# The first modulation group laid out by output columns in four parts, and three units begun chunk by chunk while it loads

## The chip, the cores and the metric

The kernel runs on one core of a Trainium2 chip. The metric is the device time of one execution in microseconds (us). Three runs of the kernel before gave 2286.52, 2291.09 and 2291.59 us, median 2291.09 us. The execution that the profiler recorded took 2286.39 us, of which 2284.6 us are the span of its instructions.

## The reference, cut to what matters

The reference is two stacks of transformer layers on 256 tokens of width 1024: two layers of a first kind, then two of a second. The change touches the beginning of the first layer alone:

```
c_act = silu(c)                                     # one vector of 1024
mod   = c_act @ w_mod[l] + b_mod[l]                 # [1024] @ [1024, 6144]
sh1, sc1, g1, sh2, sc2, g2 = split(mod, 6)
h = rms(x, ln1[l]) * (1 + sc1) + sh1                # x is [256, 1024]
p = h @ w_in[l]                                     # then heads, attention, output projection
```

So nothing of `h` can be had before `sh1` and `sc1` (the first 2048 columns of `mod`, 8 MB of float32 weights), and nothing of `p` before `h`. Each element of `h` in chunk k (128 of the 1024 features) needs only the 128 columns of `sh1` and the 128 columns of `sc1` that belong to chunk k, but over all 1024 rows of `w_mod`.

## The kernel before, in words

Activations lie transposed: features on the 128 partitions, in KC = 8 chunks, and the T = 256 tokens along the free axis. Weights come as **units**, 128 output columns by all 1024 rows (512 KB). A unit is loaded in two halves (the two queue entries of `unit(v)`, L1699) into RAW, which holds two units; ScalarE makes its high part WH, half by half (`split_high`, L2178); VectorE makes the low part WL of the first half (`split_low`, L2436) and GpSimd that of the second (`low`, L1778). A unit's product is then 24 matmuls: WH by the high and the low part of `h`, and WL by the high part. The ring of WH and WL holds four units. The loads are all issued by SyncE (SP) in one written order, and each load waits there until what lies in its place has been used: unit v waits until units up to v-2 have both low parts (`lo_done` at least v-1, half by half), from unit 2 on; nothing behind it in the list is issued before.

**The modulation.** Its weights are read in steps of 128 rows by 2048 columns, each in two halves of 512 KB. One group is 8 steps: 2048 output columns. In `modulate` (L1849) a half gives two matmuls of 512 columns, each with the 32-wide stationary operand `c_act` of its chunk repeated, so that the four matmuls of a step write four strips of 32 partitions of PSUM bank 7. `extract` (L2507) turns the bank with one transpose, adds the bias (L2516) and makes the gains A1 (L2526). The halves 0 to 15, the leading group, have places of their own in SBUF and need not wait. Halves 16 and 17 stand on SP's list behind unit 5, and TensorE uses them (`modulate` of step 8) behind unit 3.

**The beginning of the first layer, before.** SP issues: the vectors c, halves 0 to 3, common constants, x, parameters P1, halves 4 to 11, units 0 and 1, halves 12 to 15, then units 2 and 3, the large constants (1088 KB) and unit 4 and so on. TensorE: the modulation of halves 0 to 3, the sum of squares (`norm_sums`, L1950, 8 matmuls in float32), halves 4 to 15, then `units_begun` for units 0 and 1 (L1882, L1883, and L1888 with the low part of `h`), unit 2, the first rotation (L2004), unit 3, step 8 of the modulation, and the pair of units 4 and 5. ScalarE: squares of x (L2233), the root (L2227, L2229), the high parts of units 0 and 1, the eight chunks of the high part of `h` (H1, L2247), then the high parts of units 2 and 3. VectorE: the refinement of the root (L2463 to L2467), the low parts of units 0 and 1, `extract(0)`, the eight scaled chunks (L2497), and the eight low chunks of `h` (L2493), with the low part of unit 2 behind chunk 3 and that of unit 3 behind chunk 7.

A float32 matmul is shown as two records of two passes each; the matmuls of the units are one pass and one record.

Of the kernel before, what the change touches and what calls it, by code (L numbers as in the profile page):

```python
# [57 lines left out]
BEGINNING = (2, 3)  # L58
# [85 lines left out]
def build(nc, stream, mods, consts, consts2, par1, par2, lam, ccols, xT, ctxT, outT):  # L144
# [147 lines left out]
    late_full = lead_full[4:]  # L292
    mod_used, group_read, mods_ready = (sem(n) for n in ("mod_used", "group_read", "mods_ready"))
# [1373 lines left out]
    def _(sp):  # L1667
        def modulation(s):

            for half in range(2):  # L1670
                modulation_half(2 * s + half)

# [51 lines left out]
        for s in range(2):  # L1724
            modulation(s)
        sp.dma_start(C[:, 0:COMMON_W], consts[:, 0:COMMON_W]).then_inc(common_in, 16)
        sp.dma_start(X, xT).then_inc(x_in, 16)
        sp.dma_start(P1[:, :, :], par1).then_inc(common_in, 16)
        for s in range(2, LEAD - 2):
            modulation(s)  # L1730
        for v in range(2):
            unit(v)
        for s in range(LEAD - 2, LEAD):
            modulation(s)
        for l in range(DEPTH):
            for v in range(PER):
                if l or v >= 4:
                    unit(l * PER + v)
                for h in halves_behind(l, v):
                    modulation_half(h)  # L1740
                if l == 0 and v == 1:
                    for x in (2, 3):
                        unit(x)
                    sp.dma_start(C[:, COMMON_W:COMMON_W + FIRST_W], consts[:, COMMON_W:]).then_inc(consts_in, 16)
                if l == 0 and v == IN_UNITS + WO_UNITS + 1:
                    sp.dma_start(P2[:, :, :], par2).then_inc(later_in, 16)
                if l == DEPTH - 1 and v == IN_UNITS + WO_UNITS + 24:
# [73 lines left out]
    def _(pe):  # L1821
        def modulate(s):
# [6 lines left out]
            for half in range(2):  # L1829
# [21 lines left out]
                last.then_inc(mod_used, 1)  # L1851
        def unit_wait(base, i, j):
# [85 lines left out]
        def first_layer(l):  # L1938
# [3 lines left out]
            def norm_sums(half):  # L1942
                index = 2 * l + half
                pe.wait_ge(common_in, 32)
                if index:
                    pe.wait_ge(sq_added, index)
                    pe.matmul(PS[:, 6, 0:T], ones, SQ[:, 0, :], start=True, stop=False)
                for k in range(KC - 1 if index else 0, KC):
                    pe.wait_ge(sq_done, index * KC + k + 1)
                    last = pe.matmul(PS[:, 6, 0:T], ones, SQ[:, k, :], start=(k == 0), stop=(k == KC - 1))  # L1950
                last.then_inc(sum_done, 1)

            if l == 0:
                for s in range(2):
                    modulate(s)
            norm_sums(0)
            for s in range(NORM_STEPS):
                if l:
                    modulate(at + s)
            if l == 0:  # L1960
                for s in range(2, LEAD):
                    modulate(s)
# [56 lines left out]
            for x in range(IN_UNITS):  # L2019
                if x in (VALUES, VALUES + 2):  # L2020
                    token_pair(base, 0, x, H1, 0, 2)
                elif x == 0:
                    units_begun([(base + y, H1, T) for y in range(BEGINNING[l])], 2 * l)
                elif x >= BEGINNING[l] and not VALUES < x < VALUES + 4:
                    unit(x)
                if x == 2:
                    if l == 0:
                        pe.wait_ge(consts_in, 16)
                    rotate(0)
# [140 lines left out]
    def _(act):  # L2170
# [64 lines left out]
        def norm(l, half):  # L2235
# [5 lines left out]
            if half == 0 and l == 0:  # L2241
                for u in range(2):
                    split_high(u, 0, 1)
# [185 lines left out]
    def _(dve):  # L2429
# [51 lines left out]
        def norm(l, half):  # L2481
            dve.wait_ge(rstd_done, 2 * l + half + 1)
            refined(RS[:, 1, :], RS[:, 0, :], PS[:, 6, 0:T], 1.0 / D)
            if l == 0 and half == 0:
                for u in range(2):
                    split_low(u, 0, 1)
                dve.wait_ge(common_in, 32)
                extract(0)

# [6 lines left out]
            for k in range(KC):  # L2496
                dve.scalar_tensor_tensor(NX[:, k, :], X[:, k, :], A1[:, l, half, k:k + 1], RS[:, 1, :],  # L2497
                                         ALU.mult, ALU.mult).then_inc(nx_done, 1)
            for k in range(KC):
                low(k)  # L2500
                if l == 0 and half == 0 and k % 4 == 3:
                    split_low(2 + k // 4, 0, 1)
# [80 lines left out]
        def first_layer(l):  # L2583
# [76 lines left out]
            for x in range(IN_UNITS):  # L2660
                next_low(base, 0, x)
                if x == 2:
# [301 lines left out]
def _modulations(a):  # L2964
# [3 lines left out]
    steps = strips.transpose(2, 0, 1, 4, 3, 5).reshape(STEPS, P, 4, 4 * P)  # L2968
    rows = np.ascontiguousarray(a["w_mod"][1].T).reshape(BESIDE * KC, 2, P, D).transpose(0, 2, 1, 3)
# [61 lines left out]
```

## Time and profile before

| | us |
|---|---|
| three runs | 2286.52, 2291.09, 2291.59 |
| profiled execution, its own time | 2286.39 |
| its span | 2284.6 |
| TensorE busy | 2208.7 (97%) |
| VectorE / ScalarE / GpSimd busy | 1258.5 / 1109.8 / 726.9 |

The page gives each engine's busy time over the span, the busy share in 40 slices, the queues, and the chain of work that ended last. The first slice of TensorE is the only one under 80% (7 tenths). The change lies within the first 60 us, so the rows below come mostly from there: the timeline (start, duration, engine, line, operation, what was written and read, count, and in brackets the idle time before it and what released it), and the table of windows.

### The profile page before, as it was taken

Reading aid. Unit: us, or ns where it says so; the run is one execution under the profiler, and the core shown is the slowest. Engines: PE = TensorE matmul, PEld = TensorE weight load, DVE = VectorE, ACT = ScalarE, POOL = GpSimd, SP = SyncE. Lnnn points to the kernel's source line nnn. Section 1 sums busy time; section 2 is a strip of 40 time slices with the busy share of each in tenths; the row PEclk is TensorE's granted clock in tenths of the full one; section 3 lists DMA queues with packets and bytes.
Section 4 is the critical chain, followed back from the end, with each engine's and each line's share of the span. In section 5 each row is a group of like instructions: output and inputs, shape, how many; then the busy total and the mean of one; then the engine's idle time right before and its main releaser. Section 6 shows DMA issues by size and latency. Waiting matters only on the chain.

```text
span 2284.6 us, 41129 instructions
## 1 busy us (share of the span) xinstructions
PE 2208.7 (97%) x14780; PEld 1931.1 (85%) x14780; DVE 1258.5 (55%) x2278; ACT 1109.8 (49%) x2323; POOL 726.9 (32%) x563
## 2 busy tenths in 40 slices
PE   7999999999999999999999999999989999999999
PEld 4869998869998888878887688888879889787999
DVE  3767668776446645531344764363465664437564
ACT  3465554565455444532355653232343665647553
POOL 2404554414664221122221012222223235221443
PEclk9999999999999999999999999999999999999999
DMA  8766997675775322123222113223223335222554
GB/s 304 233 236 216 321 333 295 207 258 172 243 241 175 93 83 65 56 87 93 79 74 70 33 47 101 92 65 101 92 74 116 101 114 168 83 84 65 168 162 148
DMA packets 159893, 328.47 MB, mean 144 GB/s; under 512 B 17808, under 2 KB 21136, under 8 KB 159632
## 3 DMA queue, kind: packets, MB, share of 16 engines
q1 hardware_dynamic: 159616, 325.80, 43.6%
q8 instruction: 89, 1.46, 0.3%
q0 software_dynamic: 144, 0.85, 0.1%
q14 instruction: 44, 0.36, 0.1%
HBM read 325.53 MB, written 1.05 MB: 143 GB/s over the span
## 4 chain that ended last, share of the span: by engine, by line
PE 78%; issue 8%; DVE 5%; POOL 4%; ACT 2%; DMA 1%; SPq 1%; POOLq 0%; DVEq 0%; ACTq 0%
PE PS L1868 16%; PE PS L1869 15%; PE PS L1870 15%; PE PS L1913 4%; PE PS L1915 4%; PE PS L1914 4%; POOL WL L1778 3%; PE PS L737 2%; PE PS L717 2%; PE PS L1849 1%; POOL AR L1798 1%; PE PS L1932 1%; PE PS L1931 1%; PE PS L1930 1%; PE PS L751 1%
## 5 line engine op out<-in xcount | busy, mean ns | idle before, releaser
L1778 POOL TENSOR_TENSOR WL<-RAW,WH 128x512 fp32r<-128x512 f32 x434 | 598.2, 1379 | 1453.6 <-ACT WH L2178 1301.3
L1868 PE MATMUL PS<-AR,WH 128*128 128x256 f32 (+1 forms) x2632 | 857.4, 326 | 4.0 <-DVE AR L1626 1.9
L1869 PE MATMUL PS<-AR,WH 128*128 128x256 f32 (+1 forms) x2632 | 844.5, 321 | 0.0
L1870 PE MATMUL PS<-AR,WL 128*128 128x256 f32 (+1 forms) x2632 | 843.8, 321 | 0.0
L2178 ACT ACTIVATE WH<-RAW 128x512 fp32r<-128x512 f32 x840 | 492.0, 626 | 326.2 <-PE PS L1870 172.3
L2436 DVE TENSOR_TENSOR WL<-RAW,WH 128x512 fp32r<-128x512 f32 x434 | 357.2, 823 | 454.2 <-ACT WH L2178 452.2
L1868 PEld LDWEIGHTS PS<-AR,WH 128*128 128x128 f32 x2632 | 496.5, 189 | 54.6 <-issue 8.1
L1869 PEld LDWEIGHTS PS<-AR,WH 128*128 128x128 f32 x2632 | 496.8, 189 | 41.3 <-issue 2.4
L1870 PEld LDWEIGHTS PS<-AR,WL 128*128 128x128 f32 x2632 | 496.7, 189 | 40.0
L1913 PE MATMUL PS<-WH,AR 128*128 128x256 f32 x768 | 219.3, 286 | 0.0
L1915 PE MATMUL PS<-WH,AR 128*128 128x256 f32 x768 | 216.2, 282 | 0.0
L1914 PE MATMUL PS<-WL,AR 128*128 128x256 f32 x768 | 216.1, 281 | 0.0
L1913 PEld LDWEIGHTS PS<-WH,AR 128*128 128x128 f32 x768 | 144.6, 188 | 3.6 <-issue 3.0
L1914 PEld LDWEIGHTS PS<-WL,AR 128*128 128x128 f32 x768 | 144.7, 188 | 0.7 <-issue 0.5
L1915 PEld LDWEIGHTS PS<-WH,AR 128*128 128x128 f32 x768 | 144.5, 188 | 0.0
L1931 PE MATMUL PS<-AR,WH 128*128 128x256 f32 x352 | 99.1, 281 | 0.0
L1930 PE MATMUL PS<-AR,WH 128*128 128x256 f32 x352 | 99.1, 281 | 0.0
L1932 PE MATMUL PS<-AR,WL 128*128 128x256 f32 x352 | 99.0, 281 | 0.0
L1038 ACT ACTIVATE WORK<-PS 128x512 f32<-128x512 f32 (+1 forms) x48 | 23.5, 490 | 129.8 <-PE PS L1870 129.6
L1100 ACT ACTIVATE WORK<-PS,BC,QN 128x512 f32<-128x512 f32 (+1 forms) x96 | 66.9, 705 | 8.8 <-DVE BC L1502 8.8
L1500 DVE TENSOR_REDUCE BC<-PS 128x2 f32<-128x1024 f32 (+1 forms) x48 | 50.1, 1044 | 36.0 <-PE PS L717 36.0
L1932 PEld LDWEIGHTS PS<-AR,WL 128*128 128x128 f32 x352 | 66.3, 188 | 0.0
(309 smaller groups left out, 3060.9 us busy)
## 6 DMA issues: line engine op xcount, KB each, us to landing
RAW<-stream SPq DMA_DIRECT2D x868, 256.0 KB, 3.0
WORK<-mods SPq DMA_DIRECT2D x144, 512.0 KB, 5.9
WORK<-stream SPq DMA_DIRECT2D x68, 256.0 KB, 5.1
C<-consts SPq DMA_DIRECT2D x1, 1088.0 KB, 7.4
XX<-xT SPq DMA_DIRECT2D x1, 1024.0 KB, 10.2
XX<-ctxT SPq DMA_DIRECT2D x1, 1024.0 KB, 7.3
outT<-XX SPq DMA_DIRECT2D x8, 128.0 KB, 1.9
C<-consts POOLq DMA_DIRECT2D x1, 832.0 KB, 7.0
```

Source lines behind the costliest of these rows:

```text
L1778: pool.tensor_tensor(WL[:, u % 4, cut, :], raw(u, 1), WH[:, u % 4, cut, :].bitcast(f32), ALU.subtract).then_inc(lo_done[1], 1)
L1868: pe.matmul(out, WH[:, u % 4, k, :], moving[:, 0, k, :], start=(k == 0), stop=False)
L1869: pe.matmul(out, WH[:, u % 4, k, :], moving[:, 1, k, :], start=False, stop=False)
L1870: last = pe.matmul(out, WL[:, u % 4, k, :], moving[:, 0, k, :], start=False, stop=(k == KC - 1))
L1913: pe.matmul(out, still[:, 0, k, cut], WH[:, both, k, :], start=(k == 0), stop=False)
L1914: pe.matmul(out, still[:, 0, k, cut], WL[:, both, k, :], start=False, stop=False)
L1915: last = pe.matmul(out, still[:, 1, k, cut], WH[:, both, k, :], start=False, stop=(k == KC - 1))
L1930: pe.matmul(PS[:, b, 0:T], WH[:, u % 4, k, :], HID[:, 0, kk, :], start=(kk == 0), stop=False)
L1931: pe.matmul(PS[:, b, 0:T], WH[:, u % 4, k, :], HID[:, 1, kk, :], start=False, stop=False)
L1932: last = pe.matmul(PS[:, b, 0:T], WL[:, u % 4, k, :], HID[:, 0, kk, :], start=False, stop=(kk == FC - 1))
L2178: act.activation(WH[:, u % 4, cut, :], raw(u, half), ACT.Copy).then_inc(hi_done, 1)
L2436: dve.tensor_tensor(WL[:, u % 4, cut, :], raw(u, 0), WH[:, u % 4, cut, :].bitcast(f32), ALU.subtract).then_inc(lo_done[0], 1)
```

## The change

The weights of the leading group are laid out anew in memory: in four parts of four halves, where part p holds the columns of chunks 2p and 2p+1 of `sh1` and `sc1` (512 columns) over all 1024 rows. So each half holds two row chunks of 512 columns, and each gives eight matmuls of 128 columns, four per row chunk, in place of two of 512. Each part has a PSUM bank (7, 4, 5, 7), a transpose of 128 by 128, and its own small additions.

```
-BEGINNING = (2, 3)
+BEGINNING = (3, 3)
+PAIRS = KC // 2
+PAIR_BANK = (7, 4, 5, 7)
+BEHIND_CHUNK = {1: (0, 1), 3: (2,), 7: (3,)}
...
 SP:
-        for s in range(2):
-            modulation(s)
+        sp.dma_start(X, xT).then_inc(x_in, 16)
         sp.dma_start(C[:, 0:COMMON_W], consts[:, 0:COMMON_W]).then_inc(common_in, 16)
-        sp.dma_start(X, xT).then_inc(x_in, 16)
         sp.dma_start(P1[:, :, :], par1).then_inc(common_in, 16)
-        for s in range(2, LEAD - 2):
-            modulation(s)
-        for v in range(2):
-            unit(v)
-        for s in range(LEAD - 2, LEAD):
-            modulation(s)
+        for p, behind in enumerate(((0, 1), (2,), (), (3,))):
+            for h in range(4 * p, 4 * p + 4):
+                modulation_half(h)
+            for v in behind:
+                unit(v)
...
                 if l == 0 and v == 1:
-                    for x in (2, 3):
-                        unit(x)
...
 TensorE:
+        def pair(p):
+            if p == PAIRS - 1:
+                pe.wait_ge(pair_read, 1)
+            for h in range(4 * p, 4 * p + 4):
+                if h < 4:
+                    pe.wait_ge(mod_full[h], 16)
+                else:
+                    pe.wait_ge(lead_full[h - 4], 16)
+                for x in range(2):
+                    k = 2 * (h % 4) + x
+                    still = CA[:, 0, k:k + 1].broadcast_to([P, STRIP])
+                    for a in range(4):
+                        last = pe.matmul(PS[a * STRIP:(a + 1) * STRIP, PAIR_BANK[p], 0:P], still,
+                                         LEADING[h][:, x, a * P:(a + 1) * P], start=(k == 0), stop=(k == KC - 1))
+                last.then_inc(mod_used, 1)
+
+        def start_chunk(u, k):
+            if k == 0:
+                unit_wait(u, 0, 0)
+            pe.wait_ge(nhi_done, k + 1)
+            out = PS[:, u, 0:T]
+            pe.matmul(out, WH[:, u, k, :], H1[:, 0, k, :], start=(k == 0), stop=False)
+            pe.matmul(out, WL[:, u, k, :], H1[:, 0, k, :], start=False, stop=False)
+            pe.wait_ge(norm_done, k + 1)
+            return pe.matmul(out, WH[:, u, k, :], H1[:, 1, k, :], start=False, stop=(k == KC - 1))
+
+        def start():
+            norm_sums_first()
+            pair(0)
+            pair(1)
+            for k in (0, 1):
+                for u in (0, 1):
+                    start_chunk(u, k)
+            pair(2)
+            for k in (0, 1):
+                start_chunk(2, k)
+            for k in (2, 3, 4, 5):
+                for u in range(3):
+                    start_chunk(u, k)
+            pair(3)
+            for u in range(3):
+                for k in (6, 7):
+                    last = start_chunk(u, k)
+                last.then_inc(unit_done, 1)
...
+                elif x == 0 and l == 0:
+                    start()
...
-                if x == 2:
+                if x == (2 if l else 3):
                     if l == 0:
                         pe.wait_ge(consts_in, 16)
                     rotate(0)
...
 ScalarE, norm(0, 0):
-            if half == 0 and l == 0:
-                for u in range(2):
-                    split_high(u, 0, 1)
             for k in range(KC):
                 ... (the high part of chunk k)
-            if half == 0 and l == 0:
-                for u in range(2, 4):
-                    split_high(u, 0, 1)
+                if half == 0 and l == 0:
+                    for u in BEHIND_CHUNK.get(k, ()):
+                        split_high(u, 0, 1)
...
 VectorE, norm(0, 0), behind the refinement of the root:
+            if l == 0 and half == 0:
+                dve.wait_ge(common_in, 32)
+                for p in range(PAIRS):
+                    pair_columns(p)
+                    for k in (2 * p, 2 * p + 1):
+                        scaled(k)
+                    for k in (2 * p, 2 * p + 1):
+                        low(k)
+                        for u in BEHIND_CHUNK.get(k, ()):
+                            split_low(u, 0, 1)
+                return
...
+        def pair_columns(p):
+            dve.wait_ge(mod_used, 4 * (p + 1))
+            ... (transpose of 128x128 out of PAIR_BANK[p], the bias added to 2x2 columns, 2 columns of A1)
```

`norm_sums_first` is the sum of squares as before. GpSimd's list is unchanged. VectorE's first `rope(0)` moves behind the low part of one more unit, as the rotation does on TensorE; in the second layer (l = 1) nothing changes.

## Rows read from the trace of the kernel before

**Rows 1.** The page: span, TensorE's busy time, and the ending chain by engine.

```profile
span 2284.6 us, 41129 instructions
...
PE 2208.7 (97%) x14780; PEld 1931.1 (85%) x14780; DVE 1258.5 (55%) x2278; ACT 1109.8 (49%) x2323; POOL 726.9 (32%) x563
...
PE 78%; issue 8%; DVE 5%; POOL 4%; ACT 2%; DMA 1%; SPq 1%; POOLq 0%; DVEq 0%; ACTq 0%
```

**Rows 2.** Timeline of the first 35 us, all engines.

```profile
13.91 2.56 ACT L2233 ACTIVATE WORK<-XX 128x256 f32<-128x256 f32 x8 [11.30 <-DMA XX<-xT]
...
14.47 5.38 PE L1950 MATMUL PS<-WORK,C 128*128 128x256 f32 x16 [3.08 <-ACT WORK L2233]
...
19.78 3.05 PE L1849 MATMUL PS<-WORK,CA 128*32 128x512 f32 x24
...
21.76 0.43 DVE L2467 SCALAR_TENSOR_TENSOR WORK<-WORK 128x256 f32<-128x256 f32 x1
...
26.25 2.94 POOL L1778 TENSOR_TENSOR WL<-RAW,WH 128x512 fp32r<-128x512 f32 x2 [25.80 <-ACT WH L2178]
...
28.11 4.88 PE L1849 MATMUL PS<-WORK,CA 128*32 128x512 f32 x16 [2.73 <-DMA WORK<-mods]
...
31.93 0.14 PEld L1849 LDWEIGHTS PS<-WORK,CA 128*32 128x32 f32 x4 [1.08 <-DMA WORK<-mods]
33.11 0.72 DVE L2507 STREAM_TRANSPOSE WORK<-PS 128x512 f32<-128x512 f32 x1 [5.04 <-PE PS L1849]
...
34.28 3.25 DVE L2497 SCALAR_TENSOR_TENSOR WORK<-XX,A,WORK 128x256 f32<-128x256 f32 x8
34.80 3.30 ACT L2247 ACTIVATE AR<-WORK,M 128x256 fp32r<-128x256 f32 x8 [7.37 <-DVE WORK L2497]
```

**Rows 3.** Timeline from 35 to 47 us, all engines.

```profile
35.45 0.55 PE L1882 MATMUL PS<-AR,WH 128*128 128x256 f32 x1 [2.46 <-ACT AR L2247]
...
38.57 0.37 PE L1882 MATMUL PS<-AR,WH 128*128 128x256 f32 x1
...
39.21 3.06 POOL L1778 TENSOR_TENSOR WL<-RAW,WH 128x512 fp32r<-128x512 f32 x2 [10.02 <-ACT WH L2178]
...
39.64 3.71 DVE L2493 SCALAR_TENSOR_TENSOR AR<-WORK,M,AR 128x256 fp32r<-128x256 f32 x4
...
43.28 0.68 DVE L2436 TENSOR_TENSOR WL<-RAW,WH 128x512 fp32r<-128x512 f32 x1
...
44.11 1.14 ACT L2178 ACTIVATE WH<-RAW 128x512 fp32r<-128x512 f32 x2
```

**Rows 4.** SP's queue in the timeline: issues of loads.

```profile
39.75 0.33 SPq L1699 DMA_DIRECT2D RAW<-stream  x1
...
43.98 0.80 SPq L1699 DMA_DIRECT2D RAW<-stream  x2
...
45.30 0.43 SPq L1689 DMA_DIRECT2D WORK<-mods  x1
```

**Rows 5.** Timeline of TensorE around step 8 of the modulation.

```profile
50.94 0.28 PE L1869 MATMUL PS<-AR,WH 128*128 128x256 f32 x1
51.05 0.28 PE L1870 MATMUL PS<-AR,WL 128*128 128x256 f32 x1
51.26 1.05 PE L1849 MATMUL PS<-WORK,CA 128*32 128x512 f32 x4
52.50 1.05 PE L1849 MATMUL PS<-WORK,CA 128*32 128x512 f32 x4 [0.18 <-DMA WORK<-mods]
53.48 0.39 PE L1913 MATMUL PS<-WH,AR 128*128 128x256 f32 x1
```

**Rows 6.** Windows of TensorE alone: us, busy (records), granted clock, DMA share, GB/s.

```profile
29.30:31.90 2.60, 2.60 (x10) 0.50 1.02 403
...
37.00:38.50 1.50, 1.50 (x9) 0.50 0.00 0
```

**Rows 7.** Timeline of TensorE: a burst of very small matmuls in a later layer.

```profile
797.75 1.15 PE L551 MATMUL PS<-C,WORK 4*128 4x4 f32 x16
```

More of the change, by code:

```diff
@@ L292, in build @@
     late_full = lead_full[4:]
+    pair_read = sem("pair_read")
     mod_used, group_read, mods_ready = (sem(n) for n in ("mod_used", "group_read", "mods_ready"))
@@ L1667, in _ @@
     def _(sp):
-        def modulation(s):
-            for half in range(2):
-                modulation_half(2 * s + half)
         def modulation_half(h):
@@ L1851, in modulate, with norm_sums_first @@
                 last.then_inc(mod_used, 1)
+        def pair(p):
[40 more added lines that the diff above has]
+                last.then_inc(unit_done, 1)
+        def norm_sums_first():
+            pe.wait_ge(common_in, 32)
+            for k in range(KC):
+                pe.wait_ge(sq_done, k + 1)
+                last = pe.matmul(PS[:, 6, 0:T], ones, SQ[:, k, :], start=(k == 0), stop=(k == KC - 1))
+            last.then_inc(sum_done, 1)
         def unit_wait(base, i, j):
@@ L1943, in norm_sums @@
                 index = 2 * l + half
[L1944 to L1958, printed above, removed]
+                pe.wait_ge(sq_added, index)
+                pe.matmul(PS[:, 6, 0:T], ones, SQ[:, 0, :], start=True, stop=False)
+                pe.wait_ge(sq_done, index * KC + KC)
+                pe.matmul(PS[:, 6, 0:T], ones, SQ[:, KC - 1, :], start=False, stop=True).then_inc(sum_done, 1)
+            if l:
+                norm_sums(0)
+                for s in range(NORM_STEPS):
                     modulate(at + s)
-            if l == 0:
-                for s in range(2, LEAD):
-                    modulate(s)
             def unit(x):
@@ L2483, in norm @@
             refined(RS[:, 1, :], RS[:, 0, :], PS[:, 6, 0:T], 1.0 / D)
[L2484 to L2488, printed above, removed]
             def low(k):
@@ L2494, in low, with scaled @@
                                          H1[:, 0, k, :].bitcast(f32), ALU.add, ALU.subtract).then_inc(norm_done, 1)
-            for k in range(KC):
+            def scaled(k):
                 dve.scalar_tensor_tensor(NX[:, k, :], X[:, k, :], A1[:, l, half, k:k + 1], RS[:, 1, :],
                                          ALU.mult, ALU.mult).then_inc(nx_done, 1)
+            if l == 0 and half == 0:
[9 more added lines that the diff above has]
+                return
+            for k in range(KC):
+                scaled(k)
             for k in range(KC):
                 low(k)
-                if l == 0 and half == 0 and k % 4 == 3:
-                    split_low(2 + k // 4, 0, 1)
+        def pair_columns(p):
+            dve.wait_ge(mod_used, 4 * (p + 1))
+            columns, bank = slice(4 * p, 4 * p + 4), PAIR_BANK[p]
+            turned = dve.transpose(MT[:, columns, :].rearrange("p m r -> p (m r)"), PS[:, bank, 0:P])
+            if p < PAIRS - 1:
+                turned.then_inc(pair_read, 1)
+                dve.wait_ge(pair_read, p + 1)
+            else:
+                turned.then_inc(group_read, 1)
+                dve.wait_ge(group_read, 1)
+            cut, bias, gain = slice(2 * p, 2 * p + 2), PAR1["bmod"], PAR1["ln1"] + 2 * p
+            halves = lambda x: x.rearrange("p (h k) -> p h k", h=2)
+            chain(dve.tensor_tensor(halves(M1[:, 0, 0:16])[:, :, cut], halves(MT[:, columns, 0]),
+                                    halves(P1[:, 0, bias:bias + 16])[:, :, cut], ALU.add))
+            chain.wait()
+            chain(dve.scalar_tensor_tensor(A1[:, 0, 0, cut], M1[:, 0, KC + 2 * p:KC + 2 * p + 2], 1.0,
+                                           P1[:, 0, gain:gain + 2], ALU.add, ALU.mult))
+            chain.wait()
         def extract(g):
@@ L2661, in first_layer @@
                 next_low(base, 0, x)
-                if x == 2:
+                if x == (2 if l else 3):
                     rope(0)
@@ L2968, in _modulations @@
     steps = strips.transpose(2, 0, 1, 4, 3, 5).reshape(STEPS, P, 4, 4 * P)
+    pairs = wide[:, 0:2 * D].reshape(PAIRS, 2, P, 2, PAIRS, 2, 4, STRIP).transpose(4, 0, 2, 1, 6, 3, 5, 7)
+    steps[0:KC] = pairs.reshape(2 * KC, P, 2, 4 * P).reshape(KC, 2, P, 2, 4 * P).transpose(
+        0, 2, 1, 3, 4).reshape(KC, P, 4, 4 * P)
     rows = np.ascontiguousarray(a["w_mod"][1].T).reshape(BESIDE * KC, 2, P, D).transpose(0, 2, 1, 3)
```

## The prediction

> **What bounds the kernel now.** The page comes first: 97% of the span TensorE is busy and 78% of the ending chain is its own work [rows 1], so a change must take time out of TensorE's list or let it start earlier. Then the timeline of the first 60 us. TensorE does no matmul of a unit before 35.45 us [rows 3]. Until 33.0 it waits for the leading modulation group: halves 12 to 15 arrive 1.27 us apart (28.11 to 31.93, three steps), and the windows show 403 GB/s at a DMA share of 1.02 [rows 2, 6]. That stretch is bound by the transfers. From 33.11 the chain is serial: one transpose and two small operations until 34.28, eight scaled chunks, and from 35.45 the matmuls of units 0 and 1, at the half rate of TensorE's clock (granted 0.50) [rows 2, 3, 6]. Then the low chunks: four of them take 3.71 us, 0.93 each, beside GpSimd's low parts of units 2 and 3 [rows 3]. The last wait that decides in this beginning is further on: half 17, issued at 45.30 behind unit 5, is used at 52.50 with 0.18 us of idle time before it, and the pair of units 4 and 5 starts at 53.48 behind it [rows 4, 5]. Unit 5 in turn was held on SP until VectorE had made the low part of unit 3 (43.28 to 43.96) [rows 3, 4]. So two things must come earlier: TensorE's units, and the low part of unit 3 with the loads behind it.
>
> **The loads.** The same bytes move, in another order. In front of half 15 stands one unit more (unit 2, 512 KB, as much as a half): 31.93 + 1.27 = 33.2 us. Counting back at 1.27: half 11 at 28.1, unit 2 at 23.0, half 7 at 21.8, half 3 at 14.2; x, now first, by about 6 and the parameters by 8 instead of 14.4 (bounds 6 and 10; the sums move with them, but half 3 does not). SP now stands at unit 2 until the low part of unit 0 is made, with halves 8 to 15 behind it. That part: sums of squares 8.0 + 5.4 = 13.4; the refined root 2.3 later, as now (19.85 to 22.2), 15.7; first part's columns 0.7 (below), two scaled chunks and their high parts, 17.7; the high part of unit 0, 0.57 a half, 18.8; GpSimd's low part 1.5, 20.4 [rows 2, 3]. What has been issued by then keeps the queues busy until 23.0, so I take this wait at nothing, with 2 us of cover. If the cover is gone, every us of delay moves halves 8 to 15, and all behind them, by one.
>
> **TensorE's modulation.** Before, a step of four matmuls on four strips takes 3.05/3 = 1.02 us [rows 2]; the strips run side by side. After, a row chunk is the same four strips with 128 columns, a quarter: 0.26 us, 2.0 us a part, 8.2 in all, as before, but in 128 matmuls instead of 32. Below the arrival rate (0.5 us a half against 1.27). The other end: the burst of small matmuls has 16 records in 1.15 us, 0.07 each [rows 7]; a row chunk has 8 records, 0.57 us, 4.6 a part, still below 1.27 a half, but 2.6 us later where a part's data lie waiting. I take 0.26, the nearer row: the same operation with the same operands. The Trainium skill has a rule for each end (TensorE: Matmul & The Clock Gate, "Wait — 56ns, not 53.3ns?"): a start-to-start floor of about 25 ns, and about 62 ns a matmul where the sequencer decodes in software. By the first the part would take an estimated 1.7 us, by the second 4.0. No row shows 128 columns on four strips, so the trace decides nothing between them yet.
>
> **TensorE between parts 2 and 3.** Part 2 is done at 28.1 + 0.6 = 28.7, at the half rate 29.0. Then 6 matmuls of unit 2 and 36 of chunks 2 to 5. At the half rate a matmul takes (38.57 - 35.45)/14 = 0.22 us, at the full one 0.12 (50.94 to 51.05) [rows 3, 5]. Before, the clock stood at 0.50 in this same place (29.3 to 31.9) and rose after some 3 us of work, in both places where it was low [rows 6, 3]. So 14 matmuls at 0.22 and 28 at 0.12: 6.4 us, until 35.3 (all at full rate: 33.7; all low: 38.2). Chunks 4 and 5 are ready at 31.5 and wait for nobody. Part 3 lies ready since 33.2: 2.0 us. **End of part 3, E = 37.3** (35.6 to 40.2; with the 0.57 of above 39.9).
>
> **Behind E.** The transpose of 128 by 128 is between nothing and the 0.72 of 128 by 512; I take 0.3. With the two small operations (34.28 - 33.11 - 0.72 = 0.45) the columns cost 0.75. Two scaled chunks at 0.41 and the high part of chunk 7 end at E + 2.1, its low part at E + 2.6 [rows 2]. The matmuls behind it (12 of units 1 and 2, at 0.12 to 0.22) end at E + 4.2 to 5.3. Unit 3: high parts E + 2.1 to 3.2, GpSimd's low part, 1.3 to 1.5 us, at E + 4.7 [rows 3]. So unit 3 runs from about E + 4.9 = 42.2 to 45.1, and the rotation until 45.6. Before, unit 3 ended at 51.2 [rows 5]. So far 6 us would be won.
>
> **What is late next.** Behind unit 3 comes step 8 of the modulation, with halves 16 and 17. SP issues them behind unit 5, whose second half waits for GpSimd's low part of unit 3, E + 4.7. So half 17 goes out at E + 5.7 = 43.0, against 45.30: 2.3 us earlier, not 6. It took 7.2 us from there to its use [rows 4, 5], and the loads around it (unit 5, unit 6 and half 16) are the same at about the same distances, so I leave it at 7.2: 50.2, against 52.50. TensorE stands idle from 45.6 until half 16 comes, about 49, and again a little before half 17. Idle stretches of 2.5 us and more stand before both low stretches of the clock here (12.0 to 14.4 and 33.0 to 35.4 [rows 2, 3]), so I expect the matmuls behind to start at the half rate: between 0 and 14 matmuls of the pair at 0.22 instead of 0.12 and up to 0.9 us in half 17's own matmuls; 0.8 taken. Gain at the start of the pair: 2.3 - 0.8 = **1.5 us**.
>
> **What remains.** From there on every wait is relative to TensorE (evictions, low parts, the issues behind them), and I find no load that is due at a fixed time; the gain stays as it is. The first rotation moved costs nothing: it stood on TensorE's path before (0.43 us, between units 2 and 3), now it lies in the wait for half 16. On VectorE the rope behind it is one low part later, with more than 4 us until it is needed by the key scores. The low chunks 6 and 7 no longer run beside GpSimd: 0.41 instead of 0.93, inside the sum. Sum against the profiled execution: 2286.4 - 1.5 = 2284.9. The median of the runs shown lies 4.7 us above that execution, so 2291.1 - 1.5 = **2289.6 us**. About 0.2% (4.6 us) is what a measurement of this kernel can tell from no change.
>
> **Rivals.**
>
> A. *The gain comes through.* Clock at full rate behind part 2 (E = 35.6), and half 17 lands after 5 us instead of 7.2. For it: the queues lie idle for some us before (0 to 2 loads outstanding), so little stands in front. Against it: 7.2 us was measured with an idle queue before it too (windows after 37.0 show 0 GB/s [rows 6]). Gain 2.3 + 1.7 + 2.2 = 6.2 without cooling, 5 to 6 us: 2285.5.
>
> B. *Slower: SP stuck at unit 2.* One mechanism: the low part of unit 0 comes later than about 21 us, the queues run dry, and halves 8 to 15 are late. For it: the chain to it is long (x, sums at the half rate, root, a part's columns, ScalarE's halves), each term from a row in another setting; if the matmuls of part 0 go at 0.57 a chunk it comes 2 us later by itself, and part 3 takes 2.6 more. Against it: 2 us of cover. Price: E later by the delay beyond the cover; the gain of 1.5 is gone from 1.5 us of delay on. With 2 us of delay and 2.6 in part 3: 3.1 us slower, 2294.2. The pace of 62 ns in the skill's page, above, would lead here.
>
> C. *Nothing.* The half-rate clock lasts longer than 14 matmuls behind part 2 and again behind the idle time (E = 38.5, 1.5 us of cooling): 2291.0.
>
> D. *It does not do what it says*: the units are begun early, but part 3 stands behind the 42 matmuls in TensorE's order, and with all of them at the low rate E is 40.2, no earlier than the units' end is now: 0.6 us lost at half 17 and 0.8 by the clock, 1.4 us slower, 2292.5.
>
> **From this the numbers.** Forecast (gain 0.5 to 3.5) 0.45; A 0.2; B 0.17; C 0.1; D 0.08. Faster by over 0.2%: nearly all of A and a little of the forecast where the gain reaches its end, 0.22. Slower by over 0.2%: B where its delays add up, and the tail of D, 0.14. Within: 0.64. Range: from A's 2285.5 to B's 2294.2, drawn in by half a us above for the tails left out: 2285.0 to 2293.8.
>
> **What would show it.** Right: half 15 used near 33.2 with no hole in the DMA share between 20 and 33; matmuls of units 0 and 1 from about 22; a row chunk of the modulation at 0.26; part 3 behind 42 unit matmuls, E near 37; TensorE idle for 3 us before step 8 with the wait on the mods; half 17 issued near 43. Wrong: a DMA share well under 1 around 23 us (B); no idle time before step 8 (A, then the gain is 5 us or more); a clock at 1.00 throughout 28 to 36; or a pair of units 4 and 5 that starts before 49 us.

## The result, and the profile after

The kernel after takes 2294.39 us (median of 20 runs, 2290.59 to 2305.64), the one before 2289.03 us (20 runs, 2284.11 to 2292.52): ratio 1.0026, 95% interval [1.0017, 1.0035]. It is slower by 5 to 6 us (the interval gives 4 to 8); forecast were 2289.6 us and a range up to 2293.8. The profiled execution took 2294.35 us, 8 us more than that of before, which lay 3 us under its kernel's median of 2289.03.

The page first: span, TensorE and its weight loads, the loads of instruction lists (q8; 89 before), the ending chain. To be compared with [rows 1].

```profile
span 2292.5 us, 41518 instructions
...
PE 2212.2 (96%) x14972; PEld 1942.0 (85%) x14972; DVE 1263.0 (55%) x2287; ACT 1111.6 (48%) x2323; POOL 728.2 (32%) x563
...
q8 instruction: 90, 1.47, 0.3%
...
PE 67%; issue 17%; POOL 7%; DVE 4%; ACT 3%; DMA 2%; POOLq 0%; SPq 0%; DVEq 0%; ACTq 0%
```

TensorE has 192 matmul records more and is busy 3.5 us longer. The timeline of the new beginning (start, duration, engine, line):

```profile
13.63 1.95 PE L1859 MATMUL PS<-WORK,CA 128*32 128x128 f32 x64
...
16.08 0.32 DVE L2553 STREAM_TRANSPOSE WORK<-PS 128x128 f32<-128x128 f32 x1
...
19.37 2.95 POOL L1772 TENSOR_TENSOR WL<-RAW,WH 128x512 fp32r<-128x512 f32 x2 [18.91 <-ACT WH L2220]
...
20.67 0.79 SPq L1698 DMA_DIRECT2D RAW<-stream  x1
20.81 1.08 PE L1859 MATMUL PS<-WORK,CA 128*32 128x128 f32 x16 [0.18 <-DMA WORK<-mods]
21.50 4.51 SPq L1686 DMA_DIRECT2D WORK<-mods  x8
21.82 0.58 PE L1869 MATMUL PS<-AR,WH 128*128 128x256 f32 x1
...
26.21 1.08 PE L1859 MATMUL PS<-WORK,CA 128*32 128x128 f32 x16 [1.46 <-DMA WORK<-mods]
...
31.59 1.08 PE L1859 MATMUL PS<-WORK,CA 128*32 128x128 f32 x16 [0.21 <-DMA WORK<-mods]
32.60 0.58 PE L1869 MATMUL PS<-AR,WH 128*128 128x256 f32 x1
```

SP issues halves 8 to 15 from 21.50 on, behind unit 2's two issues, the second of which waited for GpSimd's low part of unit 0 (19.37 + 1.28 = 20.65); half 7, the last load in front of them, was used at 20.81. Half 8 is then used at 26.21 and half 11 at 31.59. The windows of TensorE (us, busy, granted clock, DMA share, GB/s) show the hole:

```profile
15.60:19.20 3.60, 1.29 (x32) 1.00 1.03 420
19.20:23.00 3.80, 3.27 (x37) 0.50 0.66 194
23.00:25.50 2.50, 1.75 (x9) 0.50 0.89 292
25.50:32.60 7.10, 4.25 (x64) 0.50 1.01 372
32.60:36.30 3.70, 3.70 (x21) 0.51 1.04 415
36.30:39.40 3.10, 3.10 (x27) 1.00 1.01 412
```

And the timeline of the beginning's end, beside [rows 4, 5]:

```profile
39.40 1.95 PE L1859 MATMUL PS<-WORK,CA 128*32 128x128 f32 x64
41.42 0.32 DVE L2553 STREAM_TRANSPOSE WORK<-PS 128x128 f32<-128x128 f32 x1 [5.99 <-PE PS L1859]
...
43.25 0.39 PE L1869 MATMUL PS<-AR,WH 128*128 128x256 f32 x1 [1.90 <-ACT AR L2286]
...
44.72 2.73 POOL L1772 TENSOR_TENSOR WL<-RAW,WH 128x512 fp32r<-128x512 f32 x2 [17.85 <-ACT WH L2220]
...
46.16 0.36 PE L1918 MATMUL PS<-AR,WH 128*128 128x256 f32 x1 [0.18 <-POOL WL L1772]
...
46.41 0.91 SPq L1688 DMA_DIRECT2D WORK<-mods  x2
...
51.28 1.05 PE L1843 MATMUL PS<-WORK,CA 128*32 128x512 f32 x4 [1.17 <-DMA WORK<-mods]
...
52.53 1.05 PE L1843 MATMUL PS<-WORK,CA 128*32 128x512 f32 x4 [0.20 <-DMA WORK<-mods]
...
53.52 0.39 PE L1963 MATMUL PS<-WH,AR 128*128 128x256 f32 x1
```

The pair of units 4 and 5 starts at 53.52, before at 53.48 [rows 5]. So two questions stand apart: why the beginning gives nothing, and where 5 to 8 us go after it, where the two programs are the same. Aligned by TensorE's matmuls from the end of the program, after is behind before by 0.04 us at 53.5 us, 0.9 at 199, 2.8 at 370, 4.5 at 450, 5.7 at 725, 7.6 at 740 and 7.9 at the end: in this execution hardly anything is lost behind 760 (in a second profile of after, 5.0 us at 760 and 6.9 at the end).

### The profile page after: what moved, and what is told of

Same layout as the page of the kernel before. It is cut to its first block, busy times and chain, and to the rows that moved or that the text cites. A ratio compares the mean times of both kernels' runs of the same rounds, so it can differ in the third digit from the quotient of the medians.

```text
span 2292.5 us, 41518 instructions
## 1 busy us (share of the span) xinstructions
PE 2212.2 (96%) x14972; PEld 1942.0 (85%) x14972; DVE 1263.0 (55%) x2287; ACT 1111.6 (48%) x2323; POOL 728.2 (32%) x563
## 4 chain that ended last, share of the span: by engine, by line
PE 67%; issue 17%; POOL 7%; DVE 4%; ACT 3%; DMA 2%; POOLq 0%; SPq 0%; DVEq 0%; ACTq 0%
PE PS L1918 14%; PE PS L1920 14%; PE PS L1919 14%; POOL WL L1772 5%; PE PS L1963 3%; PE PS L1965 3%; PE PS L1964 3%; DMA RAW<-stream 2%; PE PS L721 1%; ACT WH L2220 1%; PE PS L741 1%; PE PS L1982 1%; PE PS L1980 1%; PE PS L1981 1%; POOL AR L1792 1%
## 5 line engine op out<-in xcount | busy, mean ns | idle before, releaser
L2475 DVE TENSOR_TENSOR WL<-RAW,WH 128x512 fp32r<-128x512 f32 x434 | 363.9, 839 | 447.7 <-ACT WH L2220 445.8
L1918 PEld LDWEIGHTS PS<-AR,WH 128*128 128x128 f32 x2624 | 496.2, 189 | 53.9 <-issue 7.9
L1919 PEld LDWEIGHTS PS<-AR,WH 128*128 128x128 f32 x2624 | 495.9, 189 | 40.8 <-issue 2.2
L1920 PEld LDWEIGHTS PS<-AR,WL 128*128 128x128 f32 x2624 | 495.3, 189 | 40.0
L1980 PEld LDWEIGHTS PS<-AR,WH 128*128 128x128 f32 x352 | 66.7, 190 | 0.0
```

What stands on the lines that cost most here:

```text
L1918: pe.matmul(out, WH[:, u % 4, k, :], moving[:, 0, k, :], start=(k == 0), stop=False)
L1919: pe.matmul(out, WH[:, u % 4, k, :], moving[:, 1, k, :], start=False, stop=False)
L1920: last = pe.matmul(out, WL[:, u % 4, k, :], moving[:, 0, k, :], start=False, stop=(k == KC - 1))
L1980: pe.matmul(PS[:, b, 0:T], WH[:, u % 4, k, :], HID[:, 0, kk, :], start=(kk == 0), stop=False)
L2475: dve.tensor_tensor(WL[:, u % 4, cut, :], raw(u, 0), WH[:, u % 4, cut, :].bitcast(f32), ALU.subtract).then_inc(lo_done[0], 1)
```

## The experiments

Each is timed together with the kernel before (whose medians were 2288.4 to 2290.8), and the ratio, with its 95% interval, is to that. "At the pair" is the start of the pair of units 4 and 5 against 53.48 of before, from the profile.

**The two kernels again, and before with small matmuls.** Both unchanged; and before with the leading group's matmuls cut into four of 128 columns:

```diff
-last = pe.matmul(PS[at:at + STRIP, 7, :], still, ring[:, x, :], ...)
+for c in range(4):
+    last = pe.matmul(PS[at:at + STRIP, 7, c * P:(c + 1) * P], still, ring[:, x, c * P:(c + 1) * P], ...)
```

> The kernel before, unchanged. In the two profiles the pair of units 4 and 5 starts at 53.48 us before and at 53.52 after, so the beginning won and lost nothing; the 8 us come later: the matmuls of the feed-forward and down stages of the first two layers follow each other at 118.7 ns before and at 120.0 ns after (some 3.9 us in all), and single waits and clock levels between 400 and 735 us bring the rest. Theory CODE (TensorE's longer list of instructions sets the 120.0 ns, the same in each execution of a kernel): this profile shows 118.7 ns there again, median within 1 us of before. Theory CHANCE (the spacing is drawn anew in each execution): 118.7 or 120.0 in either stage, and the profile's time goes with it, 2 us a stage.

> The changed kernel, unchanged. CODE: 120.0 ns in both feed-forward stages again, 5 us slower than before (ratio 1.002 to 1.003). CHANCE: 118.7 in one or both of the stages in this profile; the timed runs still 5 us slower only if something else is lost each time, which the profile then has to show. Beginning: pair of units 4 and 5 at 53.5 +- 1 us.

> The kernel before with its layout and order, only the leading group's matmuls issued as 128 matmuls of 128 columns in place of 32 of 512 (one part of the change alone; the output is the same). CODE: TensorE's list is as much longer as in the changed kernel, so the feed-forward stages go at 120.0 ns and the kernel is about 4 us slower than before (2293). CHANCE: within 1 us of before on average. Beginning, by both: a half takes 0.5 to 1.1 us of TensorE as long as the transfers set the pace, so the first matmul of unit 0 comes at 35.5 +- 0.5 us.

Before again: 2289.15 us, 1.0000 [0.9988, 1.0012]. After again: 2299.47, 1.0043 [1.0029, 1.0057]. Before with small matmuls: 2295.5, 1.0024 [1.0014, 1.0034]: it is as slow as after, although its beginning lost only 1.43 us at the pair. The rest goes later, as in after. After once more, one run:

> The changed kernel once more, for a third profile of its beginning. In its timed runs the mean granted clock is 0.988 to 0.989 against 0.992 of the kernel before; 0.003 of 2290 us at half the rate is 7 us, all of the loss. The matmul spacing of 120.0 ns was in one of its two profiles only, so CODE is out. Theory COLD: the additional low stretches lie in the first 50 us, where TensorE has little to do between the parts: here 10 us or more of clock 0.50 before 45 us. Theory LATER: the low stretches lie behind 100 us, at single waits of the attention and stage changes (120, 195, 540, 730, 840 us), and the beginning has no more of them than the kernel before (3 to 10 us).

2295.74 us; at the pair +0.66. The feed-forward matmuls of the first layer stood 118.7 ns apart here, in after again and in before with small matmuls, and 120.0 ns in the profile of after. The same program shows both, so that spacing (2 us a stage) isn't fixed by the instruction list, as the theory CODE had it: before with small matmuls has CODE's time without its spacing.

**Unit 2's loads behind half 9 instead of half 7**, so that SP's wait has two halves more in front of it:

```diff
-for p, behind in enumerate(((0, 1), (2,), (), (3,))):
+for h in range(2 * LEAD):
+    modulation_half(h)
+    for v in {3: (0, 1), 9: (2,), 15: (3,)}.get(h, ()):
+        unit(v)
```

> The changed kernel with unit 2's loads on SP's list behind half 9 instead of half 7. In the changed kernel SP stood at unit 2 until 21.0 us, the queues ran dry and half 11 came at 31.6 instead of the forecast 28.1, half 15 late too. Theory STALL (the early gain was lost there): half 11 at 28.0 to 28.5, part 3 of the modulation ends near 38 instead of 41.35, half 17 goes out 3 us earlier and the pair of units 4 and 5 starts 2 to 3 us earlier, near 51; time 2 to 3 us under the changed kernel's (ratio to before 1.001). Theory ORDER (TensorE's 42 matmuls at the low clock in front of part 3 hold it anyway): part 3 ends less than 1 us earlier. CODE: feed-forward stages at 120.0 ns as in the changed kernel, because TensorE's list is the same.

2292.24 us, 1.0004 [0.9987, 1.0020]. The issues of the halves behind unit 2, part 3 and the pair in its timeline, and a window of TensorE:

```profile
20.42 4.04 SPq L1686 DMA_DIRECT2D WORK<-mods  x6
...
35.59 1.95 PE L1858 MATMUL PS<-WORK,CA 128*32 128x128 f32 x64
...
49.76 0.39 PE L1962 MATMUL PS<-WH,AR 128*128 128x256 f32 x1
```

```profile
20.00:25.00 5.00, 4.80 (x52) 0.52 1.03 397
```

The hole is gone (DMA share 1.03), part 3 comes 3.8 us earlier than in after, and so does the pair, 3.7 us ahead of before. The stall is shown as the cause in the beginning. How much of it reaches the time is not told well: the medians of the two kernels lie 2.2 us apart, their ratios 5 us, and the interval here is 3.8 us to either side.

**TensorE kept warm.** After with one thrown-away float32 matmul of 256 columns ahead of each wait for halves 4 to 11:

```diff
+if 4 <= h < 12:
+    pe.matmul(PS[:, 3, 0:T], ones, SQ[:, h % 4, :], start=True, stop=True)
```

> The changed kernel, with one float32 matmul of 256 columns into the unused bank 3 in front of the wait for each of halves 4 to 11 (eight matmuls whose result nobody reads), so that TensorE is not idle between the halves. COLD: no low stretch between 18 and 36 us; the 42 matmuls in front of part 3 take 5.0 instead of 9 us, part 3 ends near 38 instead of 41.35, the pair of units 4 and 5 starts 2 to 3 us earlier, mean clock 0.991, and the kernel is no slower than the one before (ratio 0.999 to 1.001). LATER: the beginning is 2 to 3 us shorter in the profile, but the timed runs stay at clock 0.989 and 1.002 to 1.004.

2291.4 us, 1.0004 [0.9992, 1.0016]; 2.3 us ahead of before at the pair, and no low clock in the profile before 190 us. Part of the beginning is the clock's.

**Two further steps.** Upon the kernel with unit 2 behind half 9: halves 16 and 17 issued ahead of unit 4, behind the large constants; then also part 3 ahead of chunks 4 and 5 (both edits shown in part):

```diff
+if 2 * LEAD <= h < 2 * LEAD + 2:
+    sp.wait_ge(mod_used, h - 15)
...
-for k in (2, 3, 4, 5): (units 0 to 2)
+for k in (2, 3): (units 0 to 2)
 pair(3)
+for k in (4, 5): (units 0 to 2)
```

> The changed kernel with unit 2 behind half 9 (as in after_unit2), and with halves 16 and 17 issued right behind the large constants, ahead of unit 4, waiting only for the first uses of their places. In after_unit2 the pair of units 4 and 5 starts at 49.8, 1.5 to 2 us after TensorE has asked for half 16. If that wait sets the pair's start: step 8 follows the rotation without a pause, the low part of unit 5 is next (its load goes out behind unit 3's low part, as before, plus 5 us), and the pair starts near 48.5, 1 to 1.5 us earlier. If unit 5 comes just as late: same start as in after_unit2, with the wait now on GpSimd's low part. Time: 0 to 2 us under after_unit2.

> As after_mods, and with part 3 of the modulation on TensorE in front of the 18 matmuls of chunks 4 and 5 instead of behind them. Theory ORDER (the 18 matmuls hold part 3 and with it unit 3's low part and unit 5's load): part 3 ends at 35 to 36 (after its last half lands, about 33, and 24 matmuls), unit 5's second half goes out near 40, the pair of units 4 and 5 starts near 46 to 47, 7 us before the kernel before; ratio 0.997 to 0.999. LATER: the beginning gains its 7 us, but the time is only 2 us under before or the same, with a mean clock of 0.989.

2291.16 us, 0.9997 [0.9986, 1.0008] and 2290.28 us, 0.9993 [0.9980, 1.0005]. In the profiles the pair starts at 46.12 and 45.73, 7.4 and 7.8 us earlier than before (forecast 48.5 for the first), but the times are only 0.7 and 1.6 us under before: 6 to 7 us are lost behind the pair. The two profiled executions, 0.8 and 7 us over their kernels' medians, have lost 11 and 16 us by 760 us. So whatever takes after's 5 to 8 us takes these too.

**The instruction list.** TensorE's list is loaded in packets of 16 KB (q8); between two fetches lie mostly 100 to 140 weight loads, with as many matmuls, and in some places several hundred (there TensorE runs loops: before has 52 branch records). A float32 matmul is two weight loads and two matmuls in the records; the change's 96 more make 384 entries, one packet and a half if a packet holds 256. The load number (records of weight loads, counted from the end of the program) at which each packet between 5000 and 5750 is fetched:

```
before, before again         5076 5185 5608 5729     5075 5185 5603 5728
after, after again, look     5123 5257 5661     5121 5257 5664     5122 5257 5664
before with small matmuls    5118 5256 5662
```

So the packets are fetched at other instructions: the one at 5729 or 5728 moves to 5661 to 5664, 64 to 68 loads further on, which with as many matmuls is some 130 entries, half a packet. The first test adds thrown-away 128-column matmuls that fill up or upset the count (32 float32 matmuls, 128 entries, half a packet):

```diff
+if 4 <= h < 12:     # before: 4 ahead of each wait; after and the last kernel: 8 ahead of halves 4 to 7
+    for a in range(4):
+        pe.matmul(PS[a * STRIP:(a + 1) * STRIP, 3, 0:P], CA[:, 0, 0:1].broadcast_to([P, STRIP]),
+                  LEADING[0][:, 0, a * P:(a + 1) * P], start=True, stop=True)
```

> The kernel before with 32 more float32 matmuls of 128 columns on TensorE, thrown away into bank 3, four ahead of each of the waits for halves 4 to 11; no other change. They lie where TensorE waits for loads anyway, so the beginning should not move by more than 0.3 us. An instruction list is loaded in pieces of 16 KB, and two of the profile's fetch gaps hold some 235 matmul and weight-load records; 32 float32 matmuls are 128 such instructions, half a piece. LIST theory (the place of the piece boundaries in TensorE's list decides how long the waits near 118, 412 and 728 us are): this kernel gets the boundaries of the split-up kernels and loses as they do: 2293 to 2296 us, 4 to 7 us over before, the wait ahead of L518 at 728 us over 2 us. Rival, no such dependence: within 1.5 us of before, the L518 wait at 1.1 us. Second rival, the loss comes with the small-column matmuls' effect on the clock: also near before, since these are few.

> The kernel after with 32 more float32 matmuls of 128 columns (thrown away into bank 3, eight ahead of each wait for halves 4 to 7). Together with the 96 that the change adds they make 512 instructions more than before, two whole pieces of 16 KB, so that the piece boundaries fall where they fell before. LIST theory: the late waits return to those of before and the time to 2289 to 2290 us, 4 to 5 under after. No dependence: within 1.5 us of after, 2292.5 to 2296. A warmer clock at 15 to 21 us alone could give back some tenths, not 4 us: the stall behind unit 2 stays.

> The same 32 matmuls in the kernel with unit 2 behind half 9, halves 16 and 17 early and part 3 ahead of chunks 4 and 5 (7 to 8 us ahead of before at the pair of units 4 and 5, yet 2290.3 us in the runs). LIST theory: the 6 us that were lost between 100 and 760 us come back and the kernel takes 2282 to 2284 us. No dependence: 2289 to 2291.5.

Before with half a packet more: 2291.73 us, 1.0013 [1.0003, 1.0023], slower (forecast 2293 to 2296, and a wait of over 2 us near 728 us; that wait is 1.27). After with two whole packets: **2288.05 us, 0.9994 [0.9984, 1.0005]**, 6 us under after. The version with the early beginning and whole packets: **2285.26 us, 0.9979 [0.9969, 0.9988]**, faster than both kernels (forecast 2282 to 2284). The packets are fetched at 5072, 5186, 5606, 5728 and 5073, 5185, 5606, 5727 in the last two, as in before, and at 5123, 5256, 5662 in the first.

**Half a packet further.** After with 64 such matmuls (two packets and a half), before with 64 (one whole packet):

```diff
-for c in range(2):     # after: 8 ahead of each of halves 4 to 7
+for c in range(4):
-for a in range(4):     # before: 4 ahead of each of halves 4 to 11
+for a in (0, 1, 2, 3) * 2:
```

> The kernel after with 64 thrown-away matmuls (16 ahead of each wait for halves 4 to 7) in place of the 32 of after_whole. With the 96 of the change they make 640 instructions more than before: two pieces and a half. All else is as in after_whole, and the clock at 15 to 21 us is if anything warmer. LIST theory: the piece boundaries fall as in after again, and the time goes back up, 2292 to 2296 us (4 to 7 over after_whole). Rival (what helped after_whole was the warm clock or the filled waiting time of the beginning, not the place of the pieces): 2287 to 2289.5.

> The kernel before with 64 thrown-away matmuls (eight ahead of each of the waits for halves 4 to 11) where before_half had 32: 256 instructions more, one whole piece of 16 KB. LIST theory: the pieces fall as in before, so 2288 to 2290 us, the same as before, although twice as many matmuls were added as in before_half, which took 2291.7. Rival (what cost before_half its 2.9 us was the added work itself, in the beginning or on the clock): at least as slow, 2291.5 to 2294.

After with the half packet: 2296.06 us, 1.0027 [1.0017, 1.0037]; 32 matmuls more in idle time cost 7 to 8 us (0.0033 by the ratios; 2288.05 and 2296.06 were timed beside 2288.87 and 2289.96 of before). Before with a whole one: 2293.07, 1.0009 [0.9999, 1.0019]; the forecast of 2288 to 2290 missed, and this kernel isn't told from the one with half a packet.

**The same with instructions that do nothing**: waits that are met long since, 128 or 256 entries (two of them in the program make one record), where TensorE waits for loads; shown is the edit of after, in before 60 and 70 of the entries stand ahead of the sums of squares:

```diff
+for _ in range(2 * {5: 20, 6: 20, 7: 20, 8: 38, 9: 15, 10: 15}.get(h, 0)):
+    pe.wait_ge(mod_full[0], 16)
```

> The kernel before with 128 more instructions in TensorE's list that do no work at all: waits that are met long since, put where TensorE waits anyway (60 ahead of the sums of squares, 68 ahead of halves 6 to 8; 0.05 us each). Half a piece of 16 KB. LIST theory: the piece boundaries move by a half and the time goes up by 2 to 6 us, to 2291.5 to 2295. Rival (extra matmul work cost before_half and before_whole their 3 us, the boundaries nothing): within 1 us of before.

> The same with 256 such waits, one whole piece. LIST theory: as before within 1 us (the waits ahead of halves 9 to 14 may cost some tenths in the beginning). Rival, any lengthening of the list costs: at least as slow as the one with 128.

> The kernel after with 128 such waits (ahead of halves 5 to 10, where TensorE is idle), so that with the change's 384 instructions more there are two whole pieces. No matmul is added and the clock of the beginning stays as low as in after. LIST theory: 2288 to 2290.5 us, the same gain over after as after_whole's 6 us less what that one had from a warmer beginning (1 us). Rival (the matmuls of after_whole helped by their work): 2293 to 2297.

Before with 128: 2292.12, 1.0016 [1.0006, 1.0026], as expected. After with 128 (two whole packets): 2289.89, 1.0006 [0.9993, 1.0019], 4.5 us under after without any added matmul. Before with 256: 2297.74, 1.0038 [1.0026, 1.0050], far off; its profile shows why: the waits themselves were not hidden. The 69 recorded ahead of the sums of squares stand 0.106 us apart, from 9.98 to 17.3 us, so the sums start at 17.62 instead of 14.47, and the pair at 61.63, 8.15 us late.

That makes the right comparison plain. From each kernel's time against before (ratio - 1, times 2289) its offset at the pair is taken; what is left was lost behind the beginning, where all run the same instructions ("after, halves early" and "best" are the first and the second of the two further steps):

```
whole packets        time   at pair   behind it
before again          0.0     +0.15      -0.1
before, 64 matmuls   +2.1     +1.27      +0.8
before, 256 waits    +8.7     +8.15      +0.5
after, 32 matmuls    -1.4     -1.15      -0.2
after, 128 waits     +1.4     -0.22      +1.6
best, 32 matmuls     -4.8     -7.96      +3.2

half packets         time   at pair   behind it
before, 32 matmuls   +3.0     +0.63      +2.3
before, 128 waits    +3.7     +0.99      +2.7
before, small        +5.5     +1.43      +4.1
after / again    +6.0/+9.8  +0.04/-0.28  +5.9/+10.1
after, 64 matmuls    +6.2     +0.45      +5.7
unit 2 behind h9     +0.9     -3.72      +4.6
after, halves early  -0.7     -7.36      +6.7
best                 -1.6     -7.75      +6.1
```

The warm kernel, at 1.6 packets, has +3.2. With whole packets the mean is 1.0 us, with half ones 5.4; the groups overlap only in the one value 3.2. In all six of the first group a packet is fetched at load 5727 to 5729, in all of the second at 5661 to 5666. A single row is good to 2 to 4 us only: the ratios' intervals are that wide, and an offset comes from one execution (three of after gave -0.28 to +0.66). So the means carry the reading, not the rows; worked out from the medians in place of the ratios they are 1.6 and 6.1, the same distance. The distance is not the same everywhere: 2.6 us among the kernels made from before, 6.5 between after and its padded versions, 3.0 in the last kernel.

A rival is the clock: over the runs of before, 0.001 less of mean granted clock goes with 1.4 to 2.0 us more, and after's clock is lower than before's (0.989 against 0.992). It doesn't divide the groups. Before with small matmuls (mean granted clock 0.9925) and before with 32 matmuls (0.9923) stand no lower than before beside them (0.992) and are 5.5 and 3.0 us slower; after with 128 waits stands at 0.9903 and is 1.4 us slower. It can be a part of what after itself loses.

**Where it is lost.** Nearly half at one place: over the profiles (one execution each), the kernels with half packets lose 5.5 us more behind the pair than those with whole ones, 2.3 of them at the change of stage near 728 us and 0.7 near 410. TensorE's first matmul there and its wait for VectorE's sum of the squares, in before, in after, in after with 128 columns x 32 more (whole), in after with 64 more (half), and in the kernel with halves 16 and 17 early (half):

```profile
727.59 1.10 PE L518 MATMUL PS<-WORK,C 128*128 128x512 f32 x2 [0.81 <-DVE WORK L2475]
```

```profile
734.47 1.10 PE L522 MATMUL PS<-WORK,C 128*128 128x512 f32 x2 [1.99 <-DVE WORK L2514]
```

```profile
728.42 1.02 PE L522 MATMUL PS<-WORK,C 128*128 128x512 f32 x2
...
730.45 0.70 PE L524 MATMUL PS<-WORK,C 128*128 128x256 f32 x2 [1.01 <-ACT WORK L2280]
```

```profile
738.40 2.04 PE L522 MATMUL PS<-WORK,C 128*128 128x512 f32 x2 [4.46 <-DVE WORK L2519]
```

```profile
731.03 2.05 PE L522 MATMUL PS<-WORK,C 128*128 128x512 f32 x2 [5.22 <-DVE WORK L2515]
```

That wait is 1.2 to 5.2 us in the ten profiles with half packets and at most 2.3 in the seven with whole ones. In the kernel with 64 matmuls more, the sum that ends it stands behind ScalarE's high parts, and these waited 1.23, 1.13 and 0.56 us for their loads just before.

The DMA view from 690 to 722 us, in after and then in after with whole packets (the first has a q8 packet in it, the second none):

```profile
q8 instruction: 1, 0.02, 0.3%
q14 instruction: 1, 0.01, 0.1%
RAW<-stream SPq DMA_DIRECT2D x25, 256.0 KB, 3.1
```

```profile
q14 instruction: 1, 0.01, 0.1%
RAW<-stream SPq DMA_DIRECT2D x25, 256.0 KB, 3.0
```

A q8 packet holds its DMA engine for 0.96 us (median over before's 89; a packet of weights 0.08 us). A load is complete when its 16 shares are: their landings lie 1.0 us apart from first to last on average over some 1000 loads without such a packet in that time, and 1.4 to 1.8 us over the 90 to 100 with one (a long landing is also likelier to meet one). That is a way in which a packet can make a load late; it is not shown that it does so here. The packet near 698 us doesn't decide alone: the wait of 4.46 us belongs to a kernel that has none between 687 and 734 us. Which packet makes which load late remains open, and so does whether a packet's place matters through the loops.

## Why the prediction was wrong, point by point

- **SP's wait at unit 2, "I take this wait at nothing, with 2 us of cover": wrong, and it is the step that failed in the beginning.** The low parts of unit 0 were forecast at 20.4. GpSimd's ended at 20.65 (19.37 + 1.28), as forecast; but a load issued behind a wait is not in the queue at that moment. Unit 2's two issues ended at 21.46, half 8's followed, and it was used at 26.21. The cover was miscounted besides: the 23.0 until which I took the queue as busy is the arrival of unit 2, which stood at the wait itself; the last load in front of the wait was half 7, by the same count at 21.8 and in the trace used at 20.81. So the queue ran down (DMA share 0.66 from 19.2 to 23.0) before the eight halves were issued (4.51 us for eight). Half 11 came at 31.59 instead of 28.1. With unit 2 behind half 9 it came at 28.34, part 3 ended at 37.5 (E was forecast at 37.3), and the 3.7 us came back.
- **x first, parameters by 8, part 0**: 7.7 to 13.7 for the sums (13.4 forecast), 2.0 us for a part of 32 matmuls: 1.95 measured. The root at 16.04 (15.7), a part's columns 0.70 (0.75). All right within 0.4 us.
- **A row chunk at 0.26 us**: 1.95/8 = 0.24, at full clock. The Trainium skill (TensorE: Matmul & The Clock Gate, "Wait — 56ns, not 53.3ns?") has about 25 ns as a floor and about 62 ns a matmul where the sequencer decodes in software; 64 records in 1.95 us are 0.030 us each, so the trace agrees with the first. (64 at 25 ns are 1.6 us, where the prediction says 1.7.)
- **42 matmuls in 6.4 us**: 32.60 to 39.40 is 6.8. The clock stood at 0.50 from 19.2 to 36.3, a longer stretch than the one forecast; it rose 3.7 us into this work. Right.
- **E = 37.3**: 41.35, 4 us late: 3.5 by the loads, 0.4 by the matmuls.
- **Unit 3 from E + 4.9**: 46.16 = E + 4.8. Right.
- **Halves 16 and 17**: half 17 issued at 46.87, not 43.0; it took 5.7 us instead of 7.2. TensorE idles 1.17 us before step 8, not 3. At the pair 0.0 instead of 1.5 us.
- **"From there on every wait is relative to TensorE; the gain stays as it is": wrong, and it is the larger failure.** After reaches the pair level with before and ends 5 to 8 us behind. A kernel 7.8 us ahead there ended 1.6 us ahead. I counted what the 96 more matmuls cost where they run and not that they shift every later end of a packet of TensorE's instruction list. The term of the sum that was missing, put at nothing, is some +4 to +6 us (4.4 between the two groups' means; 6.1 and 4.3 between after and its two versions padded to whole packets). The page shows such a term only as "q8 instruction: 89".
- **The rivals.** B had the right mechanism for the beginning (SP stuck at unit 2, queues dry), at chance 0.17; its price was worked from 2 us of delay at half 8 plus 2.6 in part 3, and its 2294.2 agrees with the measured time by accident: the delay was 3.5, part 3 cost nothing extra, and the rest came from behind the beginning. A and D did not occur; C's clock lasted longer but cost less than the stall.

What the runs settle: the stall by its undoing; that the loss behind the beginning goes with the place of the packets, by six measurements against nine, with and without added matmuls. What they don't: through which loads, and why the same shift costs kernels made from before less than after.

The Trainium skill (Runtime: NRT & Kernel Launch, "Instruction fetch mechanics") says that instructions are refilled in blocks of 16 KiB, and that crossing into the next costs little, being mostly hidden. The sizes agree (q8 packets of 16 KB); that it is hidden does not hold here, where the kernels take some 4 us of 2289 more with the boundaries half a block further.

## What to carry to other kernels

A wait on a queue that issues in order has to be covered by what is already issued behind the transfer that is running, counted from the time of the issue after the wait (here 0.56 us for each load of 512 KB) and not from the release of the wait; the load that waits does not count as its own cover. The cheap cure is to put it two places further back. When an edit changes the length of an engine's instruction list, compare it with a version padded to the same place of the 16 KB packets: otherwise a gain of 8 us in one place can read as nothing, or a neutral edit as a loss. And a gain at the beginning is measured where the beginning ends, apart from the total.

## What was not expected of the hardware

- The place of the instruction packets is worth some 4 us in 2289 (0.2%; 3 to 7 us by kernel), as much as the change under test: ratios of 0.9994 against 1.0027 for two kernels that differ by 32 thrown-away matmuls in idle time.
- Redundant waits are real instructions: the 69 recorded ahead of the sums of squares stand 0.106 us apart, 7.3 us in all, of which TensorE's idle time there hid all but 3.15.
- Matmuls of 256 columns stand 118.7 ns apart in one execution and 120.0 ns in another of the same kernel, for a whole stage. In the 18 profiles 120.0 for a whole stage was seen in three, none of them with whole packets, which is too few to tell.
